# Down projection and next projection with tiles side by side, and the norms between two transformer blocks from one pass of squares

## The chip, the cores and the metric
One core of a Trainium2 chip runs the kernel as one program. The metric is the time of one execution on the device in microseconds (us), the median of the runs shown. TensorE has two clock levels that matter here, 2.4 GHz and 1.2 GHz; the profile gives the level that the chip granted as a share of 2.4 GHz.

## What is computed
Two blocks of a model in float32, width 1024, 256 tokens (the first block has 16 meta tokens ahead of them):

```python
# first block
h = h + concat(hgrn2(u @ w_in), mamba2(u @ w_in)) @ w_out          # u = rmsnorm(h, norm1_w)
h = h + (silu(conv(gate)) * conv(val)) @ ffn_w_down                # gate, val = split(rmsnorm(h, norm2_w) @ ffn_w_up)
x = rmsnorm(h, final_norm_w)
# second block
hc = rmsnorm(ctx, pre_mix_g) * (1 + csc1) + csh1                   # 256 context tokens
hx = rmsnorm(x, pre_mix_g) * (1 + sc1) + sh1
mix = concat(conv_branch(hx @ w_in), retention(hx @ w_in, hc @ w_in)) @ w_out
x = x + g1 * rmsnorm(mix, post_mix_g)
x = x + g2 * rmsnorm(expert_choice_ffn(rmsnorm(x) * (1 + sc2) + sh2), post_ffn_g)   # 16 experts, 24 MB of weights each
```
rmsnorm(x, g) is x * g / sqrt(mean(x * x) + 1e-6). The retention's decays are log_sigmoid(ret_decay_logit), here called the decay work.

## The kernel before
The activations lie with channels on the partitions: the stream is hT, eight tiles (k = 0 to 7) of 128 channels by 272 tokens (258 from the output projection on, 256 from the down projection on; xT(k) is the last 256 tokens of tile k). Each engine has an instruction list of its own, written out by hand, and runs it in order; semaphores join them. The stages, one after the other on TensorE: input projection with both mixers beside it, output projection (tiles ob0 to ob7, oa0 to oa7), norm n2, up projection (44 tiles f0 to f43 of 8 products over k), down projection (tiles d0 to d7), norms n3 and n4, second block's input projection (28 tiles q0 to q27) with the retention between its tiles, output tiles w0 to w7, norms n5 and n6, router, and a loop over 16 experts.

Weights come through a ring of slots of 2 MB; SyncE's queue issues unit u once unit u - 5 is used (`units_used`), in the expert stage six slots are in use. An f unit holds four tiles; the down projection has six units, u_dn[cb][i], for the column halves cb = 0, 1 and the row thirds DK = (0, 8), (8, 16), (16, 22).

From the output projection to q27 every product is made of three (`split_products`, L556): the weights and the activations are split into a rounded part (hi) and the rest (lo), and TensorE adds hi*hi (L566), hi*lo (L567) and lo*hi (L570). The rounded weights are made by ScalarE (`round_weights`, L1036, instruction at L1043), chunk by chunk in the order of the list `chunks` (L386 to L408); four buffers (HB) hold them, so chunk c can be rounded once chunk c - 4 is used (`hi_used`). GpSimd makes the rest in place (L1349, its only work) and signals `w_lo`, for which TensorE waits. An f or q tile is one chunk of 8 k; a down tile k is three chunks d{k}.0, d{k}.1 (8 k each) and d{k}.2 (6 k). The activations' hi is made by ScalarE (`round_stream`, `act_round`), the rest by VectorE (L1690, L1696, L1759).

Result tiles go to three PSUM banks (TB) in the order of the list `seq`: a tile opens once the tile three before it has been read (`tiles_freed`). In the up projection ScalarE reads each tile (L1229), VectorE adds the two other taps of a convolution (L1703, L1704), ScalarE applies silu (L1232), VectorE multiplies (L1708). Added to this, at i = 13 to 20 of 22: TensorE turns the context tokens, ScalarE squares them (L1237) and takes the root (L1240), VectorE computes the gains (L1719), the decay's log chain (L1423 to L1437 at i = 19, with ScalarE's Exp and Ln at L1244, L1246), and the context rows (i = 20: reciprocal L1727, eight scalings L1729, one sum L1731).

In the output and down projections VectorE adds each finished tile to the stream (`add_tile`, L1668) and ScalarE squares it (L1212, L1253). A norm is: eight products of a matrix of 1/1024 with the squares (`norm_sum`, L575, at L581), each float32 product in two passes, the root on ScalarE (`root`, L1052), the reciprocal on VectorE (`inverse_root`, L1358), eight scalings. n2 scales at L1392. Between the blocks two norms follow each other: n3 and the scaling with the final norm's weights (L1748), ScalarE's squares of the result (L1263), n4, and the modulated scaling (L1754), whose hi part is made at L1268.

Of the kernel before, what the change touches and what calls it, by code (L numbers as in the profile page):

```python
# [148 lines left out]
def build(nc, a, out):  # L149
    with ExitStack() as ctx:  # L150
# [38 lines left out]
        eps = sb("eps", [P, 1])  # L189
# [212 lines left out]
        for k in range(KT):  # L402
            for i, (k0, k1) in enumerate(DK):
                u = u_dn[k // 4][i]
                chunk(f"d{k}.{i}", u, kcols(u, k % 4, k1 - k0))
# [15 lines left out]
        seq += [f"f{i}" for i in range(2 * FT)] + [f"d{k}" for k in range(KT)] + ["n3", "n4"]  # L421
# [3 lines left out]
        def bank_of(name):  # L425
            return ps[:, TN[name] % TB, :]
# [102 lines left out]
        def _(pe):  # L529
# [279 lines left out]
            norm_sum("n2", KEPT, lambda k: uT[:, k, 0:KEPT])  # L809
            pe.wait_ge(ev("tiles_freed"), opened[0] - 1)  # L810
            pe.nop().then_inc(ev("out_done"), 1)

            for i in range(FT):
                for s in range(2):
                    o = open_tile(f"f{2 * i + s}")
                    done(split_products(f"f{2 * i + s}", o[:, 0:KEPT], lambda k: uhi2[:, k, :], lambda k: uT[:, k, 0:KEPT],
                                        x_ready=None if i or s else 0))
# [18 lines left out]
            for k in range(KT):  # L836
                cb, m = divmod(k, 4)
                o = open_tile(f"d{k}")
                for i, (k0, k1) in enumerate(DK):
                    if k == 0:  # L840
                        pe.wait_ge(ev("ffn_act"), k1)
                    mm = split_products(f"d{k}.{i}", o[:, 0:L], lambda kk: act_hi[:, kk, :], lambda kk: act_[:, kk, :],
                                        k0, i == 0, i == 2)
                done(mm)
                if m == 3:
                    used(3)
            norm_sum("n3", L, lambda k: uT[:, k, 0:L])

            norm_sum("n4", L, lambda k: uT[:, k, 0:L])

            def in2(r):
# [3 lines left out]
                o = open_tile(f"q{r}")  # L855
                if r == 4:
                    pe.wait_ge(ev("u_tiles"), KT + 1)
                done(split_products(f"q{r}", o[:, 0:width], lambda k: hxhi[:, k, 0:width], lambda k: hx[:, k, 0:width],
                                    x_ready=None if r else 0, ready="mod_tiles"))
# [166 lines left out]
        def _(act):  # L1026
# [25 lines left out]
            def root(name, n):  # L1052

                act.wait_ge(ev("tiles_done"), TN[name] + 1)
                act.activation(bc[:, 0, 0:n], bank_of(name)[:, 0:n], ACT.Sqrt, bias=eps[:]).then_inc(ev("tiles_freed"), 1)
                act.wait_ge(ev("tiles_freed"), TN[name] + 1)
                act.nop().then_inc(ev("root"), 1)
# [82 lines left out]
            def hgrn(j):  # L1140
# [16 lines left out]
                if (j - 32) % 3 == 2:  # L1157
                    act.wait_ge(ev("hg_mean"), h + 1)

                    act.activation(hg_lf, ps[:, 7, 0:T], ACT.Sqrt, bias=eps[:]).then_inc(ev("hg_root"), 1)  # L1160
# [40 lines left out]
            act.activation(bc[:, 0, 0:T], ps[:, 3, 0:T], ACT.Sqrt, bias=eps[:]).then_inc(ev("root"), 1)  # L1201
# [12 lines left out]
            round_weights("f1")  # L1214
# [7 lines left out]
            for i in range(FT):  # L1222
                for s in range(2):
                    m = s * FT + i
                    round_weights((f"f{2 * i + s + 2}", f"d0.{s}")[i == FT - 1])
# [12 lines left out]
                if i == 18:  # L1238
                    act.wait_ge(ev("ctx_mean"), 1)
                    act.activation(bc[:, 0, L:2 * L], ps[:, 6, 0:L], ACT.Sqrt, bias=eps[:]).then_inc(ev("ctx_root"), 1)  # L1240

                if i == 19:
# [724 lines left out]
```

## Time and profile before

| | us |
|---|---|
| runs | 1841.27, 1846.86 (median), 2098.88 |
| profiled execution | 1842.59, its span 1840.7 |
| TensorE products busy in the span | 1429.5 (78%) |
| VectorE, ScalarE, GpSimd busy | 483.4, 439.1, 269.6 |
| mean granted TensorE clock | 0.876 |

Rows of the trace are in us from the start of the span. A row of the chain of waits is start, duration, engine, tensor, line. A row of the timeline is start, busy time, engine, line, operation, operands, count, and in brackets the engine's idle time before it and what ended it.

### The profile page before, as it was taken

How to read it: one execution, taken by the hardware profiler on the slowest of the kernel's cores; microseconds unless marked ns; L12 is line 12 of the kernel's file. 1: busy time of each engine (PE TensorE's matmuls, PEld its weight loads, DVE VectorE, ACT ScalarE, POOL GpSimd, SP SyncE). 2: the span in 40 equal slices, each digit the busy share in tenths (PEclk: the TensorE clock that was granted, in tenths of full speed). 3: DMA queues.
4: the chain of work that ended last, by engine and by line, in shares of the span. 5: the costliest groups of instructions: out<-in, count | busy, mean ns of one | idle time of the engine just before them, and what ended most of it. 6: DMA issues, size and time to landing. Idle time of an engine off the chain costs nothing.

```text
span 1840.7 us, 21118 instructions
## 1 busy us (share of the span) xinstructions
PE 1429.5 (78%) x8673; PEld 881.7 (48%) x8673; DVE 483.4 (26%) x917; ACT 439.1 (24%) x655; POOL 269.6 (15%) x116
## 2 busy tenths in 40 slices
PE   6999899788997879988776677666777676766675
PEld 5777676577997878886522122212222122221221
DVE  3444677644447041583200000000000000000001
ACT  2232555534655343452100000000000000000001
POOL 0000000154884745430000000000000000000000
PEclk9999999889999989999777778788787878887887
DMA  7853443323554332233299999999999999999995
GB/s 253 292 183 142 146 176 112 125 92 120 190 173 161 126 138 92 93 121 154 112 429 429 428 429 428 429 428 429 429 429 428 428 429 428 429 429 429 429 429 246
DMA packets 101115, 523.94 MB, mean 285 GB/s; under 512 B 7961, under 2 KB 30897, under 8 KB 76353
## 3 DMA queue, kind: packets, MB, share of 16 engines
q1 hardware_dynamic: 100841, 523.08, 70.1%
q8 instruction: 40, 0.66, 0.1%
q14 instruction: 18, 0.15, 0.0%
q10 hardware_dynamic: 216, 0.06, 0.0%
HBM read 522.07 MB, written 1.05 MB: 284 GB/s over the span
## 4 chain that ended last, share of the span: by engine, by line
DMA 45%; PE 39%; DVE 10%; ACT 3%; issue 2%; POOL 1%; SPq 0%; DVEq 0%; ACTq 0%; PEldq 0%
DMA ring<-in_w_down 23%; DMA ring<-in_w_up 22%; PE ps L773 8%; PE ps L566 5%; PE ps L570 5%; PE ps L567 5%; PE ps L998 3%; PE ps L1012 2%; PE ps L931 1%; PE ps L553 1%; PE ps L613 1%; DVE arena L1557 1%; PE ps L581 1%; DVE arena L1588 1%; DVE bc L1361 1%
## 5 line engine op out<-in xcount | busy, mean ns | idle before, releaser
L998 PE MATMUL ps<-ring,arena 128*32 128x512 f32 x2048 | 312.2, 760 | 136.7 <-DMA ring<-in_w_up 120.9
L1349 POOL TENSOR_TENSOR ring_r<-ring,ring_r 128x1024 fp32r<-128x1024 f32 (+1 forms) x112 | 269.4, 2418 | 546.9 <-ACT ring_r L1043 546.4
L566 PE MATMUL ps<-arena_r,ring_r 128*128 128x258 f32 (+2 forms) x880 | 271.1, 308 | 45.9 <-POOL ring_r L1349 17.2
L570 PE MATMUL ps<-arena_r,ring_r 128*128 128x258 f32 (+2 forms) x880 | 261.3, 297 | 0.0
L1012 PE MATMUL ps<-ring,arena 128*32 128x512 f32 x1024 | 175.4, 819 | 110.5 <-DMA ring<-in_w_down 103.4
L998 PEld LDWEIGHTS ps<-ring,arena 128*32 128x32 f32 x2048 | 68.7, 130 | 363.2 <-DMA ring<-in_w_up 185.6
L773 PE MATMUL ps<-uT,ring 128*128 128x272 f32 x832 | 206.2, 403 | 3.2 <-DVE uT L1392 3.2
L566 PEld LDWEIGHTS ps<-arena_r,ring_r 128*128 128x128 f32 x880 | 172.3, 196 | 56.5 <-issue 30.7
L773 PEld LDWEIGHTS ps<-uT,ring 128*128 128x128 f32 x832 | 157.7, 194 | 38.0 <-issue 7.1
L570 PEld LDWEIGHTS ps<-arena_r,ring_r 128*128 128x128 f32 x880 | 172.1, 196 | 2.8
L567 PE MATMUL ps<-arena_r,ring_r 128*128 128x256 f32 (+2 forms) x528 | 160.3, 304 | 0.0
L1012 PEld LDWEIGHTS ps<-ring,arena 128*32 128x32 f32 x1024 | 33.2, 131 | 234.8 <-DMA ring<-in_w_down 157.5
L1929 DVE TENSOR_TENSOR arena<-arena,ps 128x512 f32<-128x512 f32 x16 | 11.0, 687 | 437.2 <-PE ps L998 437.2
L1043 ACT ACTIVATE ring_r<-ring 128x1024 fp32r<-128x1024 f32 (+1 forms) x112 | 115.0, 1036 | 25.2 <-PE ps L567 14.8
L567 PEld LDWEIGHTS ps<-arena_r,ring_r 128*128 128x128 f32 x528 | 104.7, 198 | 3.8 <-issue 0.7
L567 PE MATMUL ps<-uT_r,ring_r 128*128 128x258 f32 x352 | 100.8, 286 | 0.0
L553 PE MATMUL ps<-arena 128*128 (+1 forms) x544 | 78.1, 305 | 18.9 <-DVEq L1921 18.9
L553 PEld LDWEIGHTS ps<-arena 128*128 128x128 f32 x544 | 75.6, 221 | 31.4 <-issue 31.4
L1931 DVE COPY arena<-ps 128x512 f32<-128x512 f32 x16 | 11.1, 692 | 301.3 <-PE ps L1012 301.3
L1328 ACT ACTIVATE arena<-ps 128x512 f32<-128x512 f32 x16 | 9.6, 597 | 313.0 <-PE ps L998 313.0
L1330 ACT ACTIVATE arena<-ps 128x512 f32<-128x512 f32 x16 | 9.6, 597 | 297.7 <-PE ps L1003 297.7
L1018 PE MATMUL ps<-arena 128*128 128x512 f32 x128 | 64.8, 653 | 14.3 <-DVEq L1934 14.3
(331 smaller groups left out, 1336.9 us busy)
## 6 DMA issues: line engine op xcount, KB each, us to landing
ring<-in_w_gate SPq DMA_DIRECT2D x64, 2048.0 KB, 26.0
ring<-in_w_up SPq DMA_DIRECT2D x64, 2048.0 KB, 19.7
ring<-in_w_down SPq DMA_DIRECT2D x64, 2048.0 KB, 25.7
ring<-in_w_in SPq DMA_DIRECT2D x20, 2048.0 KB, 12.1
ring<-in_w_ada SPq DMA_DIRECT2D x12, 2048.0 KB, 8.5
ring<-in_ffn_w_up SPq DMA_DIRECT2D x22, 1024.0 KB, 7.3
ring<-in_w_out SPq DMA_DIRECT2D x6, 2048.0 KB, 8.7
ring<-in_ffn_w_down SPq DMA_DIRECT2D x4, 2048.0 KB, 8.3
```

The lines of the kernel that those rows point to most:

```text
L553: mm = pe.matmul(o, l, r, start=i == 0, stop=i == len(pairs) - 1)
L566: pe.matmul(o, hi[:, k, :], r_(xhi(k0 + k)), start=first and k == 0, stop=False)
L567: mm = pe.matmul(o, hi[:, k, :], r_(xlo(k0 + k)), start=False, stop=False)
L570: mm = pe.matmul(o, lo[:, k, :], r_(xhi(k0 + k)), start=False, stop=last and k == nk - 1)
L581: mm = pe.matmul(o[:, 0:n], w[:], src(k), start=k == 0, stop=k == nk - 1)
L613: mm = pe.matmul(ps[32 * j:32 * j + 32, 3, :], cond[:, k, :], w[:, k, :], start=k < 4, stop=k >= 4)
L773: mm = pe.matmul(o[:, 0:T], w[:, k, :], uT[:, k, :], start=k == 0, stop=k == KT - 1)
L998: mm = pe.matmul(ps[32 * j:32 * j + 32, half, :], xs[:, kt, :], w[:, k, 512 * j:512 * j + 512], start=kt == 0, stop=kt == KT - 1)
L1012: mm = pe.matmul(ps[32 * j:32 * j + 32, half, :], heT[:, j, 32 * i:32 * i + 32], w[:, j, 512 * half:512 * half + 512], start=i == 0, stop= ...
L1018: mm = pe.matmul(ps[:, 4 + b, :], Gt[:, w * P:w * P + P], ye[:, half * 512:half * 512 + 512], start=False, stop=False, skip_group_check=True)
L1043: act.activation(r_(rounded(c)), chunks[c][1], ACT.Copy).then_inc(ev("w_hi"), 1)
L1349: pool.tensor_tensor(r_(w), w, f_(rounded(c)), ALU.subtract).then_inc(ev("w_lo"), 1)
```

## The change
The diff's core. It orders the down projection's chunks by `DOWN`: in each half of four tiles, three tiles side by side over the row thirds, then the fourth. f0 to f2 and q0 to q2 are computed side by side over k. The norms n2, n3 and n4 are made of two products each: VectorE adds up the squares of tiles 0 to 6, and the last tile's squares are the second product. n4 is no longer computed from the scaled stream: ScalarE squares the stream with the magnitudes of the final norm's weights as scale (small[:, 216:224]), n4 comes before n3, with 1e-12 under its root, and the gain of q's input includes those weights (small[:, 208:216]). The stream's own scaling follows after q's input. The log chain and the context rows are moved from the up projection into the down projection, the rounding of f0 to f2 ahead of n2's last squares.

```diff
+        DOWN = [(k, i) for k0 in (0, 4) for ks in (range(k0, k0 + 3), [k0 + 3]) for i in range(3) for k in ks]
...
# TensorE
-            norm_sum("n2", KEPT, lambda k: uT[:, k, 0:KEPT])
+            def last_sums(name, width, acc, last):
+                o = open_tile(name)
+                pe.matmul(o[:, 0:width], ones[:], acc, start=True, stop=False)
+                squares[0] += 1
+                pe.wait_ge(ev("squares"), squares[0])
+                done(pe.matmul(o[:, 0:width], ones[:], last, start=False, stop=True))
+            squares[0] += KT - 1
+            pe.wait_ge(ev("norm2_sums"), 1)
+            last_sums("n2", KEPT, uT[:, 0, 0:KEPT], uT[:, KT - 1, 0:KEPT])
...
+            def side_by_side(names, width, xhi, xlo, ready):
+                tiles = [open_tile(name) for name in names]
+                for k in range(KT):
+                    pe.wait_ge(ev(ready), k + 1)
+                    for name, o in zip(names, tiles):
+                        mm = split_products(name, o[:, 0:width], xhi, xlo, first=k == 0, last=k == KT - 1, ks=[k])
+                        if k == KT - 1:
+                            done(mm)
+            side_by_side(["f0", "f1", "f2"], KEPT, lambda k: uhi2[:, k, :], lambda k: uT[:, k, 0:KEPT], "u_tiles")
...
-            for k in range(KT):
-                cb, m = divmod(k, 4)
-                o = open_tile(f"d{k}")
-                for i, (k0, k1) in enumerate(DK):
...
-                if m == 3:
-                    used(3)
-            norm_sum("n3", L, lambda k: uT[:, k, 0:L])
-            norm_sum("n4", L, lambda k: uT[:, k, 0:L])
+            for k, i in DOWN:
+                if i == 0:
+                    open_tile(f"d{k}")
...
+                if i == 2:
+                    done(mm)
+                    if k % 4 == 3:
+                        used()
+                elif k % 4 == 3:
+                    mm.then_inc(ev("units_used"), 1)
+            squares[0] += 2 * (KT - 1)
+            pe.wait_ge(ev("stream_sums"), 1)
+            last_sums("n4", L, hx[:, 0, 0:L], hx[:, KT - 1, 0:L])
+            last_sums("n3", L, uT[:, 0, 0:L], uT[:, KT - 1, 0:L])
...
+                if r == 0:
+                    side_by_side(["q0", "q1", "q2"], L, lambda k: hxhi[:, k, 0:L], lambda k: hx[:, k, 0:L], "mod_tiles")
...
# ScalarE
             for k in range(KT):
+                if k >= 5:
+                    round_weights(f"f{k - 5}")
                 act.wait_ge(ev("stream_tiles"), 2 * KT + k + 1)
                 act.activation(uT[:, k, 0:KEPT], hT[:, k, KEPT0:T], ACT.Square).then_inc(ev("squares"), 1)
...
+            def stream_squares(k):
+                act.wait_ge(ev("stream_tiles"), 3 * KT + k + 1)
+                act.activation(hx[:, k, 0:L], xT(k), ACT.Square, scale=small[:, 216 + k:217 + k]).then_inc(ev("squares"), 1)
+                act.activation(uT[:, k, 0:L], xT(k), ACT.Square).then_inc(ev("squares"), 1)
+            for n, (k, i) in enumerate(DOWN):
+                round_weights(f"d{k}.{i}")
+                if n == 4:
                     act.wait_ge(ev("lg_abs"), 1)
                     act.activation(small[:, 40:48], small[:, 32:40], ACT.Exp, scale=-1.0).then_inc(ev("lg_exp"), 1)
+                if n == 6:
                     act.wait_ge(ev("lg_one"), 1)
                     act.activation(small[:, 56:64], small[:, 48:56], ACT.Ln).then_inc(ev("lg_log"), 1)
...
+                if n >= 3 and DOWN[n - 3][1] == 2:
+                    stream_squares(DOWN[n - 3][0])
+            round_weights("q2")
+            stream_squares(KT - 1)
+            root("n4", L, 0, 1)
+            root("n3", L, L)
             for k in range(KT):
                 act.wait_ge(ev("mod_scaled"), k + 1)
                 act.activation(r_(hxhi[:, k, 0:L]), hx[:, k, 0:L], ACT.Identity, bias=mod[:, k, 0:1]).then_inc(ev("u_hi"), 1)
+            act.activation(r_(hxhi[:, :, L:2 * L]), hx[:, :, L:2 * L], ACT.Copy).then_inc(ev("u_hi"), 1)
...
# VectorE
                 add_tile(f"oa{k}", k, KEPT0)
+                if 1 <= k < KT - 1:
+                    dve.wait_ge(ev("squares"), 2 * KT + k + 1)
+                    ins = tt(uT[:, 0, 0:KEPT], uT[:, 0, 0:KEPT], uT[:, k, 0:KEPT], ALU.add)
...
             for k in range(KT):
                 add_tile(f"d{k}", k, META)
+                if 1 <= k < KT - 1:
+                    dve.wait_ge(ev("squares"), 3 * KT + 2 * k + 2)
+                    st(tt(hx[:, 0, 0:L], hx[:, 0, 0:L], hx[:, k, 0:L], ALU.add))
+                    st(tt(uT[:, 0, 0:L], uT[:, 0, 0:L], uT[:, k, 0:L], ALU.add))
+                    st.wait()
+                if k == 2:
+                    context_rows()
+                if k == KT - 2:
+                    dve.nop().then_inc(ev("stream_sums"), 1)
             inverse_root(L)
-            for k in range(KT):
-                stt(xT(k), xT(k), pc("fin", k), bc[:, 1, 0:L], ALU.mult, ALU.mult).then_inc(ev("x_tiles"), 1)
-            inverse_root(L)
...
```
`context_rows` holds the lines L1726 to L1731 of before; the log chain stands just ahead of this loop.

## Rows read from the trace of the kernel before

**Rows 1.** The page: DMA share in 40 slices of the span, and GpSimd's group
```profile
DMA  7853443323554332233299999999999999999995
...
L1349 POOL TENSOR_TENSOR ring_r<-ring,ring_r 128x1024 fp32r<-128x1024 f32 (+1 forms) x112 | 269.4, 2418 | 546.9 <-ACT ring_r L1043 546.4
```

**Rows 2.** The chain of waits, two pieces of the expert stage
```profile
915.37 24.53 DMA ring<-in_w_down
...
939.95 3.35 PE ps L1012 x16
...
943.31 25.99 DMA ring<-in_w_up
```

**Rows 3.** Windows: PE, PEld, DVE, ACT, POOL busy (count), granted clock, DMA
```profile
440.00:460.00 20.00, 18.82 (x134) 18.49 (x135) 12.90 (x26) 13.57 (x22) 12.18 (x6) 0.87 0.19 60
460.00:480.00 20.00, 19.39 (x160) 19.04 (x159) 9.35 (x22) 11.74 (x21) 16.80 (x7) 1.00 0.60 204
```

**Rows 4.** The chain of waits at norm n2
```profile
429.75 3.73 PE ps L581 x16
...
434.06 1.78 DVE bc L1361
...
435.86 4.54 DVE uT L1392 x2
```

**Rows 5.** Timeline of TensorE: starts of f0, f4, f40, d0.0, d0.2, d4.2, q0, q4
```profile
440.88 0.55 PE L566 MATMUL ps<-arena_r,ring_r 128*128 128x258 f32 x1 [7.42 <-DVE uT_r L1690]
...
455.39 0.36 PE L566 MATMUL ps<-arena_r,ring_r 128*128 128x258 f32 x1 [0.30 <-PE ps L570]
...
568.89 0.36 PE L566 MATMUL ps<-arena_r,ring_r 128*128 128x258 f32 x1 [0.30 <-PE ps L570]
...
585.89 0.36 PE L566 MATMUL ps<-arena_r,ring_r 128*128 128x256 f32 x1 [0.62 <-POOL ring_r L1349]
...
599.46 0.55 PE L566 MATMUL ps<-arena_r,ring_r 128*128 128x256 f32 x1 [7.61 <-POOL ring_r L1349]
...
636.52 0.58 PE L566 MATMUL ps<-arena_r,ring_r 128*128 128x256 f32 x1 [3.34 <-POOL ring_r L1349]
...
683.48 0.36 PE L566 MATMUL ps<-arena_r,ring_r 128*128 128x256 f32 x1 [4.07 <-DVE arena_r L1759]
...
699.57 0.47 PE L566 MATMUL ps<-arena_r,ring_r 128*128 128x512 f32 x1 [0.30 <-PE ps L570]
```

**Rows 6.** Timeline of GpSimd
```profile
435.29 4.83 POOL L1349 TENSOR_TENSOR ring_r<-ring,ring_r 128x1024 fp32r<-128x1024 f32 x2 [14.29 <-ACT ring_r L1043]
...
575.29 4.67 POOL L1349 TENSOR_TENSOR ring_r<-ring,ring_r 128x1024 fp32r<-128x1024 f32 x2 [5.59 <-ACT ring_r L1043]
...
604.93 6.56 POOL L1349 TENSOR_TENSOR ring_r<-ring,ring_r 128x768 fp32r<-128x768 f32 x3 [0.94 <-ACT ring_r L1043]
...
671.74 4.84 POOL L1349 TENSOR_TENSOR ring_r<-ring,ring_r 128x1024 fp32r<-128x1024 f32 x2 [11.86 <-ACT ring_r L1043]
```

**Rows 7.** The chain of waits, log chain and context rows
```profile
577.70 2.30 DVE small L1437
...
585.20 5.76 DVE arena L1729 x8
...
590.98 2.30 DVE arena L1731
```

**Rows 8.** The chain of waits from the down projection to q0
```profile
670.56 6.32 DVE hT L1748 x5
...
680.00 1.76 DVE bc L1361
```

**Rows 9.** Timelines of VectorE and ScalarE at the last down tile
```profile
664.22 0.42 DVE L1672 TENSOR_TENSOR hT<-hT,ps 128x256 f32<-128x256 f32 x1 [7.50 <-PE ps L570]
...
664.73 0.42 ACT L1253 ACTIVATE uT<-hT 128x256 f32<-128x256 f32 x1 [6.76 <-DVEq L1674]
...
665.16 1.28 ACT L1055 ACT_TABLE_LOAD   x1
```

More of the change, by code:

```diff
@@ L420, in build @@
         seq += [f"ob{k}" for k in range(KT)] + [f"oa{k}" for k in range(KT)] + ["n2"]
-        seq += [f"f{i}" for i in range(2 * FT)] + [f"d{k}" for k in range(KT)] + ["n3", "n4"]
+        seq += [f"f{i}" for i in range(2 * FT)] + [f"d{k}" for k in range(KT)] + ["n4", "n3"]
         seq += [f"q{j}" for j in range(28)] + [f"w{k}" for k in range(KT)] + ["n5", "n6"]
@@ L1200, in _ @@
             act.wait_ge(ev("mz1_done"), 1)
-            act.activation(bc[:, 0, 0:T], ps[:, 3, 0:T], ACT.Sqrt, bias=eps[:]).then_inc(ev("root"), 1)
+            act.activation(bc[:, 0, 0:T], ps[:, 3, 0:T], ACT.Sqrt, bias=eps[:, 0:1]).then_inc(ev("root"), 1)
             m2_round(1)
@@ L1244, in _ @@
                     act.activation(small[:, 40:48], small[:, 32:40], ACT.Exp, scale=-1.0).then_inc(ev("lg_exp"), 1)
+                if n == 6:
                     act.wait_ge(ev("lg_one"), 1)
                     act.activation(small[:, 56:64], small[:, 48:56], ACT.Ln).then_inc(ev("lg_log"), 1)
-            act_round(FT - 1)
-            round_weights("d0.2")
-            for k in range(KT):
-                if k < KT - 1:
-                    round_weights(f"d{k + 1}.1")
-                act.wait_ge(ev("stream_tiles"), 3 * KT + k + 1)
-                act.activation(uT[:, k, 0:L], xT(k), ACT.Square).then_inc(ev("squares"), 1)
-                if k < KT - 1:
-                    round_weights(f"d{k + 1}.2")
@@ L1256, in _ @@
-            root("n3", L)
-            act.activation(r_(hxhi[:, :, L:2 * L]), hx[:, :, L:2 * L], ACT.Copy).then_inc(ev("u_hi"), 1)
-            round_weights("q1")
-            for k in range(KT):
-                act.wait_ge(ev("x_tiles"), k + 1)
-                act.activation(uT[:, k, 0:L], xT(k), ACT.Square).then_inc(ev("squares"), 1)
-            root("n4", L)
+                if n >= 3 and DOWN[n - 3][1] == 2:
+                    stream_squares(DOWN[n - 3][0])
+            round_weights("q2")
@@ L1366, in _ @@
             st(dve.memset(ones1[:], 1.0 / P))
[L1367 removed]
+            st(dve.memset(eps[:, 0:1], 1e-6))
+            st(dve.memset(eps[:, 1:2], 1e-12))
             st.wait()
@@ L1719, in _ @@
                         st(stt(gain[:, :, c], mod[:, 8:16, c], 1.0, pc("prem", 0, 8), ALU.add, ALU.mult))
[L1720 to L1729 removed]
                     st.wait()
[L1731 removed]
+                    st(tt(small[:, 208:216], gain[:, :, 0], pc("fin", 0, 8), ALU.mult))
             act_rest(FT - 1)
@@ L1741, in ret_args, with context_rows @@
                 dve.nop().then_inc(ev("ret_arg"), 1)
+            lgt = bcast8[:, 24:32]
+            log1p_of_exp(lgt, small[:, 40:48], small[:, 48:56], small[:, 56:64], small[:, 32:40], "lg_abs", "lg_exp", "lg_one", "lg_log")
+            st.link(stt(small[:, 80:88], lgt, 0.0, small[:, 56:64], ALU.min, ALU.subtract))
+            def context_rows():
+                dve.wait_ge(ev("ctx_root"), 1)
+                st.link(dve.reciprocal(bc[:, 1, L:2 * L], bc[:, 0, L:2 * L]))
+                for k in range(KT):
+                    st(stt(hx[:, k, L:2 * L], hx[:, k, L:2 * L], gain[:, k, 1:2], bc[:, 1, L:2 * L], ALU.mult, ALU.mult))
+                st.wait()
+                st.link(tt(hx[:, :, L:2 * L], hx[:, :, L:2 * L], mod[:, 0:8, 1:2].to_broadcast([P, KT, L]), ALU.add))
@@ L1763, in _ @@
+            dve.wait_ge(ev("root"), roots[0])
+            st.link(dve.reciprocal(bc[:, 1, L:2 * L], bc[:, 0, L:2 * L]))
+            for k in range(KT):
+                stt(xT(k), xT(k), pc("fin", k), bc[:, 1, L:2 * L], ALU.mult, ALU.mult).then_inc(ev("x_tiles"), 1)
             dve.wait_ge(ev("dist_loaded"), 16)
```

75 lines of the change are left out of this document (36 added, 39 removed).

## The prediction
> **What bounds the kernel now.** The page's slices come first. From slice 21 on the DMA engines are busy over 90% of the time, and before it they are mostly idle [rows 1]. The chain of waits says the same of its second half: a transfer of some 25 us, 3 us of TensorE, the next transfer [rows 2]. So the expert stage runs at the pace of its weights, and nothing in the diff touches it. The first 900 us are computation. At their end the ring of six slots has long been full and waits for the first expert, so whatever the first part saves, the end should save too: the same transfers start earlier. I therefore look only for the time at which TensorE reaches fixed places. The timeline of TensorE's starts gives them [rows 5]: up projection tile f0 at 440.88, f4 at 455.39, f40 at 568.89, down projection at 585.89, first tile of the next projection (q0) at 683.48, q4 at 699.57. A tile of 24 products takes 2.88 us at the full clock: from 460 to 480 us 160 products run in 20 us at granted clock 1.00, 2.4 GHz, 0.12 us each with 0.3 us every fourth tile [rows 3].
>
> **Part 1, the norm ahead of the up projection.** Before, the last output tile ends at 429.5; sixteen passes of the sum of squares (L581) take 3.73 us, the root 0.5, the reciprocal 1.78, and then two scalings take 4.54 us and hold f0 until 440.88 [rows 4, 5]. Two scalings cost 0.9 us elsewhere; here GpSimd works from 435.29 to 440.12 on f0 and f1 (4.83 us, two operations), and VectorE's second scaling ends only when it does [rows 6]. In the new kernel VectorE adds squares 0 to 6 beside TensorE's output tiles, so after the last square (at 430.4) only one product of 0.5 us is left, not eight: the root comes at 431.0 instead of 433.5. And f0, f1 and f2 are rounded during the last output tiles, so GpSimd is idle when the scaling begins. Reciprocal until 433.3, first scaling, rounding and rest 1.3 us: f0 starts at 434.7, 6.2 us earlier.
> Then f0, f1 and f2 run side by side: 72 products. TensorE idles 3.7 us ahead of them. After the old idle it ran at 1.2 GHz for 4.4 us (mean grant 0.87 from 440 to 460 [rows 3]); I take 4 us of that again: 19 products at 0.21 and 53 at 0.12, together 10.5 us, until 445.2. What is late next is f3. Its rounding stands behind f0's eviction in ScalarE's order, and f0 now ends at 444.5, last but two. Eviction 0.55, rounding 1.05, GpSimd 2.42 (the mean of its line [rows 1]): f3 starts at 448.6 and f4 at 452.0. Gain at f4: 455.4 - 452.0 = **3.4 us**. With the clock kept at 2.4 GHz it would be 5.3; with two more blocked sums in front of the norm, about 1.
>
> **Part 2, context rows and decay leave the up projection.** From f40 to the down projection the old kernel needs 585.89 - 568.89 = 17.0 us for four tiles that need 12.0. ScalarE's and VectorE's log chain stands ahead of f42's rounding, with eight-element operations of 2.3 us each [rows 7]. Without it: **5.0 us**. What it leaves behind (a product of eight gains, one more root of eight numbers) runs on engines with some 4 us of slack for a freed bank; zero, at most 2.4 us if one of them meets GpSimd and the slack is not there.
>
> **Part 3, the down projection.** Its 24 chunks are 16 of 2.88 us and 8 of 2.16 us, 63.4 us, with two hand-overs 64.0. Before, it lasts from 585.89 to 664.2, 78.3 us. The excess of 14.3 us is the start of d0.2 at 599.46 (7.6 us idle: the last activation tiles came behind the 8 us of context rows, 585.20 to 593.3 [rows 5, 7]), the wait for the last weight unit until 636.52 (3.3 us idle: all three units of the first half were given back at once), and 2.5 us of low clock after each. All of it goes. The order with three tiles side by side puts d0.2 17.3 us after the start, so the last activation tiles have time; the first unit is given back after d3.0, 22 us ahead of the transfer's use. **14.3 us.**
> But the work comes back here. The context rows (a reciprocal 1.75, eight scalings, a sum of 2.3 us) now stand on VectorE between the add of d2 and the add of d3; behind d3's add stand the bank that d6.0 wants and, on ScalarE, d3's squares and the rounding of all chunks after d6.0. In the down projection GpSimd works 6.56 us for every 7.92 us (three operations [rows 6]), and rows show what VectorE does beside it: 8-element operation 2.30 us while GpSimd runs two operations from 575.29 to 579.96 [rows 6, 7]; five of eight stream scalings 6.32 us, while GpSimd runs from 671.74 to 676.58 [rows 6, 8]. VectorE gets in one operation with two SBUF inputs per operation of GpSimd. The working, with the down projection starting at 577.5 (568.9 - 3.4 + 12.0): the tail of the log chain meets GpSimd until about 598.7, so d0 is added 1.7 us late; the first two sums of squares wait for it too; d4.0's weights come 1.5 us late. Context rows begin at 608.0, three scalings get in by 616.7 between GpSimd's three last chunks, then GpSimd has nothing (ScalarE waits for d3), the other five take 1.9 and the sum 2.3: 620.9. d3 is added at 621.4, d6.0 starts at 621.5 instead of 616.6 (4.9), and the chunk after it waits for rounding and GpSimd (1.4). Sum **-7.8 us**. Bounds: 0, if VectorE is never held (context rows then take 7 us, less than the 8.6 us of chunks in hand), and -17, if every sum and every scaling pays a whole operation of GpSimd. I take -7.8 as it follows the pattern of the rows that are nearest. The down projection then ends at 577.5 + 64.0 + 7.8 = 649.3.
> The Trainium skill says of this ("SBUF — State Buffer", section "SBUF: two separate sides") that VectorE with two SBUF inputs and GpSimd share a port pair as an exclusive lock, held for the whole instruction. It speaks against the change's place for the context rows, and the trace agrees (2.30 us for eight elements). Without such a lock this term would be 0 and the time about 1810.
>
> **Part 4, the norms between the blocks.** Before, from the last down product (664.2) to q0 (683.48): 19.3 us with two sums of squares, two roots, two reciprocals and the stream scalings between them [rows 8]. New, from that end T: add 0.3 to 0.7, squares until 1.6, table load 1.28 (the old one starts right behind the square [rows 9]), root until 3.4, reciprocal until 5.3, scaling, rounding and rest 1.7 as before (680.00 + 1.76 to 683.48): q0 at T + 7.0. GpSimd's q2 is done by T + 5, so nothing holds the scalings. **12.3 us.** q0 to q2 side by side then take 10.5 us as above, until T + 17.5; q3 again waits for eviction, rounding and GpSimd until T + 21.0; q4 starts at T + 24.3, 17.3 us after q0 where it was 16.1: **-1.1 us**. The stream's own scaling (a reciprocal and eight operations) is moved behind the products, where VectorE is free until the rotations; 0. The context's rest, 2.3 us, is done by T + 16.4, ahead of q4. The three weight units that the old kernel asks for at 664.3 are asked for from T - 5 on; they are wanted at T + 24 and later.
>
> **Sum.** 3.4 + 5.0 + 14.3 - 7.8 + 12.3 - 1.1 = 26.1 us. The profiled execution took 1842.59 (span 1840.7 and 1.9 around it): 1816.5. Two of the runs shown are 1841.27 and 1846.86 (the median, 4.3 above the profiled one), their mean 1.5 above it. Forecast: **1818 us**, a chance of 0.5; its own range 1812 to 1824.
>
> **Rivals.**
> *VectorE is not held in the down projection* (0.25). For: chunks are rounded up to four ahead, so there are gaps. Against: the 2.30 us of an 8-element operation. Time 1818 - 7.8 = 1810; with the clock kept in part 1 too, 1808.
> *The lock bites further* (0.13): sums, log chain and context rows each meet GpSimd, -17 instead of -7.8: 1827.
> *The expert transfers hide it* (0.07): the stage is bound by DMA, and if its transfers were what is full already, the end would stay: 1843. Against: slices 19 and 20 of the DMA row are 3 and 2 tenths [rows 1], so the bound begins after the first expert's start.
> *Slower than before* (0.05): ScalarE runs in order, and each stream square now stands ahead of the weights' rounding. If a tile's two sums each lose a whole operation of GpSimd (2 x 2.8), then with add, two squares, rounding and GpSimd 5.6 + 0.4 + 0.8 + 1.05 + 2.4 = 10.3 us stand against 7.9 us of products: 2.4 us on each of six tiles, 14 us; and context rows at 8 x 2.8 + 4 = 26 us against 6 us of cover lose 20 us where I count 4.9, 15 more. 1818 + 14 + 15 = 1847. It decides from the point at which GpSimd is never idle for a whole chunk; the profile shows 1.4 us of idle in 7.9.
>
> **Chances.** The range: 1806 to 1832; what stays outside is the third and fourth rival and tails. A measurement of this kernel tells about 2% from no change, 37 us, that is below 1810 or above 1884. Faster by over 2%: the first rival's better half and a little, 0.15. Slower by over 2%: 0.01. Within: 0.84.
>
> **What would show it.** f0 at about 434.7 with a last product of squares at 430.5, f3 released by GpSimd at about 448.6, f4 at 452. No wait between f40 and the down projection at 577.5. In the down projection no wait on a weight transfer, but one of some 5 us at about 617 on VectorE (d6.0, with the bank of d3), VectorE's context scalings at 2.8 us for each of the first three. The end of the down projection to q0: 7 us. Wrong would be: no wait at d6.0 (first rival), waits at several tiles (second), or a stage from f4 to f40 that is not as long as before (113.5 us), or an expert stage longer than before.

## The result, and the profile after

The changed kernel takes **1821.38 us** in the median of four runs (1820.54 to 1821.69), beside 1847.09 us for the kernel before on the same chip (four runs, 1841.27 to 2098.88): a ratio of 0.9873 with a 95% interval of 0.9854 to 0.9891, so 1.1 to 1.5% less time, inside the 2% to which the forecast gave 0.84. The ratio leaves out the one slow run, of 2098.88 us. The forecast was 1818 us with 1806 to 1832 around it. The profiled execution took 1821.69 us (span 1819.9), where the profiled one of before took 1842.59 (1840.7): 20.8 us of span, where the sum said 26.1.

The page of the changed kernel first, the DMA share in 40 slices:

```profile
DMA  7853443423654342323599999999999999999995
```

GpSimd's work is what it was in [rows 1], 112 operations of 2.42 us. The DMA row is full from slice 21 on, as before; slice 20, which had 2 tenths, has 5. The expert stage only starts earlier, with the same transfer of some 25 us, then 3 us of TensorE.

Where the time went is read from TensorE's starts (columns: start, us, engine, line, operation, in brackets the idle time ahead of it and who ended it). Changed kernel: output tiles oa4 and oa5, n2's products, f0, f3, f4, f40, d0.0, d6.0, the two norms, q0, q3, q4:

```profile
417.32 0.36 PE L567 MATMUL ps<-arena_r,ring_r 128*128 128x258 f32 x1 [0.30 <-PE ps L571]
...
421.32 0.39 PE L567 MATMUL ps<-arena_r,ring_r 128*128 128x258 f32 x1 [0.90 <-DVE hT L1704]
...
430.96 0.70 PE L813 MATMUL ps<-uT,ones 128*128 128x258 f32 x2 [0.77 <-DVE uT L1717]
...
436.61 0.55 PE L567 MATMUL ps<-arena_r,ring_r 128*128 128x258 f32 x1 [4.11 <-DVE uT_r L1728]
...
451.08 0.36 PE L567 MATMUL ps<-arena_r,ring_r 128*128 128x258 f32 x1 [3.40 <-POOL ring_r L1380]
...
456.02 0.36 PE L567 MATMUL ps<-arena_r,ring_r 128*128 128x258 f32 x1 [0.30 <-PE ps L571]
...
569.31 0.36 PE L567 MATMUL ps<-arena_r,ring_r 128*128 128x258 f32 x1 [0.30 <-PE ps L571]
...
581.54 0.36 PE L567 MATMUL ps<-arena_r,ring_r 128*128 128x256 f32 x1 [0.30 <-DVEq L1743]
...
623.25 0.58 PE L567 MATMUL ps<-arena_r,ring_r 128*128 128x256 f32 x1 [3.56 <-DVE hT L1704]
...
652.37 0.67 PE L813 MATMUL ps<-arena,ones 128*128 128x256 f32 x2 [0.30 <-PE ps L571]
...
658.88 0.36 PE L567 MATMUL ps<-arena_r,ring_r 128*128 128x256 f32 x1 [4.14 <-DVE arena_r L1804]
...
672.99 0.36 PE L567 MATMUL ps<-arena_r,ring_r 128*128 128x256 f32 x1 [3.81 <-POOL ring_r L1380]
...
677.90 0.48 PE L567 MATMUL ps<-arena_r,ring_r 128*128 128x512 f32 x1 [0.30 <-POOL ring_r L1380]
```

A product's start less its idle bracket is the end of the one before. So oa7 ends at 430.96 - 0.77 = 430.19, and the last down product, T, at 652.37 - 0.30 = 652.07. Against [rows 5]:

| stage, us | before | predicted | after |
|---|---|---|---|
| end of oa7 to f4 | 25.9 | 22.6 | 25.8 |
| f4 to f40 | 113.5 | 113.5 | 113.3 |
| f40 to d0.0 | 17.0 | 12.0 | 12.2 |
| d0.0 to T | 78.3 | 71.8 | 70.5 |
| T to q0 | 19.3 | 7.0 | 6.8 |
| q0 to q4 | 16.1 | 17.3 | 19.0 |

oa7 itself ends 0.7 us later than before. Its group of four tiles, oa4 to oa7, starts 0.5 us earlier (417.32) than in the kernel before:

```profile
417.79 0.36 PE L566 MATMUL ps<-arena_r,ring_r 128*128 128x258 f32 x1 [0.30 <-PE ps L570]
```

It lasts 430.19 - 417.32 = 12.9 us where it took 429.45 - 417.79 = 11.7: 1.2 us are lost there, most of them at oa5, which waits 0.90 us for the add that frees its bank. At q4 the gain is 699.57 - 677.90 = 21.7 us.

There are three waits of 3.4 to 3.8 us in these rows (f3, d6.0, q3); in the kernel before, f3 and d6.0 do not wait at all, and q3 waits 1.05. What follows each is in the windows of the changed kernel (columns as in [rows 3]):

```profile
623.00:627.00 4.00, 3.75 (x17) 3.76 (x18) 0.95 (x3) 3.66 (x5) 1.88 (x1) 0.50 0.54 198
627.00:632.00 5.00, 5.00 (x36) 5.00 (x35) 0.00 (x0) 0.96 (x2) 5.00 (x3) 0.77 0.01 3
...
672.90:677.90 5.00, 4.62 (x25) 4.47 (x25) 5.00 (x3) 0.51 (x2) 4.97 (x2) 0.66 0.01 3
```

TensorE works on without a gap from 623 us, but at granted clock 0.50, 1.2 GHz, for 4 us and at 0.77 for the next 5: (1 - 0.50) x 4 + (1 - 0.77) x 5 = 3.1 us on top of the wait, an estimate from the grants. For q3 the grant is 0.66 over the tile. In f3 and q3 the fall comes inside the tile: the first products of f3 start 0.12 us apart, and from 451.9 to 455.1 0.21, so the tile lasts 456.02 - 0.30 - 451.08 = 4.6 us and not 2.88.

Why f3 waits is plain from ScalarE and GpSimd. ScalarE (f0's eviction, f3's rounding), changed kernel:

```profile
447.00 0.56 ACT L1259 ACTIVATE arena<-ps,par 128x256 f32<-128x256 f32 x1 [6.12 <-PE ps L571]
447.47 1.04 ACT L1072 ACTIVATE ring_r<-ring 128x1024 fp32r<-128x1024 f32 x1
```

GpSimd, the rest of f3 and the operations beside the context rows further down, changed kernel:

```profile
448.59 2.35 POOL L1380 TENSOR_TENSOR ring_r<-ring,ring_r 128x1024 fp32r<-128x1024 f32 x1 [15.48 <-ACT ring_r L1072]
...
610.70 7.45 POOL L1380 TENSOR_TENSOR ring_r<-ring,ring_r 128x1024 fp32r<-128x1024 f32 x3 [2.68 <-ACT ring_r L1072]
```

With three tiles side by side f0 ends with the last but two of 72 products. Until then ScalarE stood 6.12 us at the eviction with f3's rounding queued behind it, and GpSimd 15.48 us.

VectorE, changed kernel: the first sum of n2, three operations of the log chain, the context rows, the add of d3:

```profile
418.70 2.10 DVE L1717 TENSOR_TENSOR uT<-uT 128x258 f32<-128x258 f32 x1 [6.96 <-ACT uT L1243]
...
586.36 2.35 DVE L1457 SCALAR_TENSOR_TENSOR small<-bcast 128x8 f32<-128x8 f32 x1
589.04 2.03 DVE L1460 TENSOR_SCALAR small<-small 128x8 f32<-128x8 f32 x1 [0.33 <-ACT small L1285]
...
595.25 0.20 DVE L1465 RECIPROCAL small<-small 128x8 f32<-128x8 f32 x1
...
612.29 8.12 DVE L1781 SCALAR_TENSOR_TENSOR arena<-arena,small,bc 128x256 f32<-128x256 f32 x8
...
622.77 0.42 DVE L1704 TENSOR_TENSOR hT<-hT,ps 128x256 f32<-128x256 f32 x1
```

The context rows stand ahead of the add that frees d6.0's bank, as forecast, and d6.0 starts 0.5 us after that add's start.

### The profile page after: what moved, and what is told of

Same layout as the page of the kernel before. It is cut to its first block, busy times and chain, and to the rows that moved or that the text cites. A ratio compares the mean times of both kernels' runs of the same rounds, so it can differ in the third digit from the quotient of the medians.

```text
span 1819.9 us, 21088 instructions
## 1 busy us (share of the span) xinstructions
PE 1420.7 (78%) x8637; PEld 874.8 (48%) x8637; DVE 508.8 (28%) x938; ACT 438.2 (24%) x655; POOL 270.0 (15%) x116
## 3 DMA queue, kind: packets, MB, share of 16 engines
HBM read 522.07 MB, written 1.05 MB: 287 GB/s over the span
## 4 chain that ended last, share of the span: by engine, by line
DMA 45%; PE 39%; DVE 10%; ACT 3%; issue 2%; POOL 1%; SPq 0%; DVEq 0%; ACTq 0%
DMA ring<-in_w_down 23%; DMA ring<-in_w_up 22%; PE ps L774 7%; PE ps L567 5%; PE ps L571 5%; PE ps L568 5%; PE ps L1027 3%; PE ps L1041 3%; PE ps L960 1%; PE ps L554 1%; PE ps L614 1%; DVE arena L1589 1%; POOL ring_r L1380 1%; DVE arena L1620 1%; PE ps L705 1%
## 5 line engine op out<-in xcount | busy, mean ns | idle before, releaser
L1982 DVE COPY arena<-ps 128x512 f32<-128x512 f32 x16 | 11.1, 692 | 303.8 <-PE ps L1041 303.8
L1359 ACT ACTIVATE arena<-ps 128x512 f32<-128x512 f32 x16 | 9.6, 597 | 314.9 <-PE ps L1027 314.9
L1361 ACT ACTIVATE arena<-ps 128x512 f32<-128x512 f32 x16 | 9.6, 597 | 293.6 <-PE ps L1032 293.6
L1363 ACT ACTIVATE arena<-ps 128x512 f32<-128x512 f32 x16 | 9.6, 597 | 279.6 <-PE ps L1041 279.6
## 6 DMA issues: line engine op xcount, KB each, us to landing
ring<-in_w_in SPq DMA_DIRECT2D x20, 2048.0 KB, 11.7
```

## The experiments

All ratios are against the kernel before, run beside each on the same chip. The unchanged opening of the program shifts by some 3 us either way from run to run (n2's products start between 428.7 and 435.2), so stages are compared by their length.

**1. The fourth tile's weights rounded ahead of f0's eviction.** The fourth buffer is free all along.

```diff
             round_stream(uhi2, 1, KEPT)
+            round_weights("f3")
...
+            round_weights("q3")
             act.activation(r_(hxhi[:, :, L:2 * L]), hx[:, :, L:2 * L], ACT.Copy)
```

> f3 and q3 are rounded ahead of the first evictions. My theory (their late weights, and the low clock after the wait, ate the side-by-side gain): f3 starts at 447.4 instead of 451.1 and runs at 0.12 us a product, f4 at 450.5 instead of 456.0; q4 some 4 to 5 us earlier on top; time 1811 to 1813. Rival (the clock is low there whatever comes before, and GpSimd only blocks VectorE elsewhere): less than 4 us in all, 1818 or more.

Measured: 1815.16 us (1813.24 to 1816.09), ratio 0.9831 (0.9809 to 0.9853). TensorE in this run, f3 and f4:

```profile
449.66 0.39 PE L567 MATMUL ps<-arena_r,ring_r 128*128 128x258 f32 x1 [1.04 <-DVEq L1745]
...
454.25 0.36 PE L567 MATMUL ps<-arena_r,ring_r 128*128 128x258 f32 x1 [1.44 <-POOL ring_r L1382]
```

End of oa7 to f4 is 23.3 us, q0 to q4 14.3. The wait on GpSimd at f3 is gone, but f3 now waits 1.0 us for f0's bank, and f4 1.4 for GpSimd. f4 comes 2.5 us earlier behind oa7 where I expected 5.5, q4 4.7 us earlier on top as expected. Part of the loss was the rounding's place; the rest stays, because f0's bank and buffer come free late anyway.

**2. f0 to f2 and q0 to q2 one after another**, all else as changed.

```diff
-            side_by_side(["f0", "f1", "f2"], KEPT, ...)
+            for nm in ("f0", "f1", "f2"):
+                side_by_side([nm], KEPT, ...)
```

and the same for q0 to q2.

> f0 to f2 and q0 to q2 one after the other, all else as changed. My theory: f0 ends at 442, so f3's weights come in time and f4 starts at about 451 (5 us earlier); q0 to q4 takes 16.1 us as before instead of 19.0; time 1813 to 1815. Rival (side by side saves the waits for k): 3 to 5 us slower, 1825.

Measured: 1811.85 us (1808.98 to 1812.04), ratio 0.9816 (0.9796 to 0.9837). ScalarE in this run, f0's eviction (f3's rounding starts right behind it, at 440.71):

```profile
440.24 0.56 ACT L1261 ACTIVATE arena<-ps,par 128x256 f32<-128x256 f32 x1 [1.64 <-PE ps L571]
```

Windows of this run, f0 to f3:

```profile
434.00:440.00 6.00, 5.82 (x24) 5.74 (x25) 4.92 (x14) 2.52 (x6) 0.00 (x0) 0.50 0.26 81
440.00:450.00 10.00, 9.70 (x80) 9.52 (x80) 3.82 (x9) 7.25 (x12) 5.90 (x3) 0.99 0.01 2
```

f0 starts at 434.18 and is evicted 6.1 us later (in the changed kernel 10.4). f3 has its weights in time, nothing waits, and the clock stays up behind f0's slow first tile. End of oa7 to f4: 21.2 us instead of 25.8; q0 to q4: 14.8 instead of 19.0. Side by side costs 4.6 + 4.2 = 8.8 us. The single step of this study that pays most is to take it out.

**3. The context rows one tile later.**

```diff
-                if k == 2:
+                if k == 3:
                     context_rows()
```

> The context rows stand behind d3's add instead of d2's. If they cost what the wait at d6.0 and the low clock after it show, this wait (3.6 us) is gone and the down projection takes 65 to 66 us instead of 70.5, time about 1816. Rival: GpSimd is never idle behind d3, the scalings take 2.8 us each, and d4's add is late instead: no change, 1821.

Measured: 1817.76 us (1817.63 to 1823.05), ratio 0.9848 (0.9827 to 0.9869). VectorE in this run:

```profile
622.62 1.75 DVE L1779 RECIPROCAL bc<-bc 128x256 f32<-128x256 f32 x1
624.40 12.54 DVE L1781 SCALAR_TENSOR_TENSOR arena<-arena,small,bc 128x256 f32<-128x256 f32 x8
636.98 4.37 DVE L1783 TENSOR_TENSOR arena<-arena,mod 128x2048 f32<-128x2048 f32 x1
```

GpSimd in this run:

```profile
615.00 20.86 POOL L1380 TENSOR_TENSOR ring_r<-ring,ring_r 128x1024 fp32r<-128x1024 f32 x9 [2.67 <-ACT ring_r L1072]
```

The window of its down projection:

```profile
585.80:651.50 65.70, 64.18 (x528) 63.50 (x528) 49.10 (x45) 32.09 (x46) 51.64 (x24) 1.00 0.47 174
```

The wait at d6.0 is gone, and with it the low clock: 65.7 us against 70.5, grant 1.00, as my theory had it. The gain is read from the stage; the ratio's interval overlaps that of the changed kernel (0.9854 to 0.9891). Yet the context rows themselves take longer, 12.5 us for eight scalings instead of 8.1, and the sum 4.4 instead of 2.3: GpSimd works without a gap until 615.00 + 20.86 = 635.86, of which 11.5 us beside the scalings, five of its operations of 2.3 us. One scaling gets in for each (11.5), and the last ones take 0.4 each. Their length is not what costs; where they stand is. From T to q0 it takes 7.9 us here (6.8).

**4. The old norm n2 put back**, and with it the old places of the rounding of f0 to f2.

```diff
-                if k >= 5:
-                    round_weights(f"f{k - 5}")
...
+            norm_sum("n2", KEPT, lambda k: uT[:, k, 0:KEPT])
```

> Norm n2 as eight products again and no early rounding of f0 to f2; the rest as changed. Old root and blocked scaling: f0 at 440.3 instead of 436.6; side by side then until 451, f4 at 459.5: 3.5 us slower, 1825. Rival (VectorE's sums held back the output tiles as much as they saved): 1821 or less.

Measured: 1833.19 us (1830.65 to 1837.13), ratio 0.9927 (0.9903 to 0.9951), 8 us above what was expected. TensorE in this run:

```profile
453.29 0.58 PE L567 MATMUL ps<-arena_r,ring_r 128*128 128x258 f32 x1 [6.07 <-POOL ring_r L1377]
```

f2 is rounded at its old place, behind f0's eviction, but side by side it is wanted with f0: TensorE waits 6.07 us in the middle of the three. So this kernel prices two things at once and says nothing of the norm; experiment 12 does it with the tiles in sequence.

**5. Log chain and context rows back in the up projection** (i = 19 and i = 20), the rest as changed.

```diff
+                if i == 19:
+                    ... log1p_of_exp(...)
+                if i == 20:
+                    ... reciprocal, eight scalings, sum
...
-                if k == 2:
-                    context_rows()
```

> Log chain and context rows back in the up projection (i = 19 and 20), the rest as changed. f40 to the down projection takes 17 us again instead of 12.2, but the down projection loses its waits (64 to 65 us instead of 70.5): 0 to 2 us faster than the changed kernel, about 1820. Rival (the move itself is a gain): 5 us slower, 1826 or more.

Measured: 1827.96 us (1827.11 to 1834.03), ratio 0.9916 (0.9887 to 0.9946). TensorE in this run, f42, d0.0, d1.0:

```profile
579.04 0.55 PE L567 MATMUL ps<-arena_r,ring_r 128*128 128x258 f32 x1 [2.90 <-POOL ring_r L1379]
...
587.16 0.36 PE L567 MATMUL ps<-arena_r,ring_r 128*128 128x256 f32 x1 [0.75 <-POOL ring_r L1379]
...
595.68 0.58 PE L567 MATMUL ps<-arena_r,ring_r 128*128 128x256 f32 x1 [5.44 <-DVEq L1742]
```

f40 to d0.0 is back at 17.0 us, as before; the 5.0 of part 2 are shown. My theory, that the down projection would give most of it back, missed: the new order opens its second tile one chunk after the first, that tile wants the bank of f42, and VectorE reads it only behind the context rows, so d1.0 waits 5.4 us. The new order needs the move; whether the move needs the new order is asked in experiment 6. By the stages the moves are worth 4.8 us ahead of d0.0 and 0.9 behind it, 6.6 us between the medians, although they bring the wait at d6.0.

**6. The down projection tile by tile again**, the rest as changed.

```diff
-        DOWN = [(k, i) for k0 in (0, 4) for ks in (range(k0, k0 + 3), [k0 + 3]) for i in range(3) for k in ks]
+        DOWN = [(k, i) for k in range(KT) for i in range(3)]
```

> Down projection tile by tile again (Ln right after Exp, for the order's sake), the units still given back one by one, the rest as changed. My theory: with the moves made, d0.2's activations are ready in time, and d3's bank is wanted three tiles later than before, so the context rows cost nothing: the down projection takes 65 us instead of 70.5, time about 1816. Rival (the side-by-side order is what removed the old stall): d0.2 waits again 5 us or more, 1821 to 1827.

Measured: 1823.03 us (1820.74 to 1826.76), ratio 0.9887 (0.986 to 0.9914). Its down projection lasts 69.6 us (70.5). TensorE in this run, d2.0 and d5.0:

```profile
598.67 0.36 PE L567 MATMUL ps<-arena_r,ring_r 128*128 128x256 f32 x1 [1.74 <-POOL ring_r L1378]
...
626.43 0.36 PE L567 MATMUL ps<-arena_r,ring_r 128*128 128x256 f32 x1 [3.29 <-POOL ring_r L1378]
```

ScalarE ahead of d3's squares, and the window of the down projection:

```profile
622.09 0.51 ACT L1277 ACTIVATE arena<-hT,small 128x256 f32<-128x256 f32 x1 [4.72 <-DVEq L1704]
...
580.86:650.42 69.56, 64.22 (x528) 63.48 (x528) 38.73 (x44) 32.94 (x47) 55.49 (x26) 1.00 0.43 155
```

Neither side had it: d0.2 did not wait for its activations, and it was not faster either. Two other waits, for GpSimd's rest of the weights, come in their place, and both lead back to the moved work. d3's products end at 614.7, but VectorE adds d3 at 621.58, behind the context rows (612.42 to 621.55); ScalarE stands 4.72 us for that add, and d5.0's rounding is next after d3's squares. In the same way d0's add (593.80) stands behind the log chain, and d2.0's rounding behind d0's squares. So the context rows cost a wait of some 3 us in this order too. No low clock follows it, though: behind the 3.29 us of idle the products start 0.12 us apart from the second on, and the grant is 1.00 over the whole stage. With the context rows out of the up projection, the order of the down projection is worth nothing that these runs resolve.

**7. The context scalings with one operand from PSUM.**

```diff
-   st(stt(hx[:, k, L:2 * L], hx[:, k, L:2 * L], gain[:, k, 1:2], bc[:, 1, L:2 * L], ALU.mult, ALU.mult))
+   st(stt(hx[:, k, L:2 * L], ps[:, 4 + k % 2, 0:L], gain[:, k, 1:2], bc[:, 1, L:2 * L], ALU.mult, ALU.mult))
```

> The eight context scalings read their data from PSUM instead of SBUF (other data, so q's context half is not the model's), so each has one SBUF tensor input less; everything else as changed. If VectorE is held because it and GpSimd both want two SBUF inputs, the eight take 3 to 4 us instead of 8.1 and the wait at d6.0 shrinks from 3.6 us to nothing, down projection 66 us. Rival (the scalings are slow for their shape, or for the sync between engines): 8 us and the wait stay.

Measured: 1812.12 us in one run, so only its trace is compared. VectorE in this run:

```profile
609.84 3.23 DVE L1781 SCALAR_TENSOR_TENSOR arena<-ps,small,bc 128x256 f32<-128x256 f32 x8
613.10 4.40 DVE L1783 TENSOR_TENSOR arena<-arena,mod 128x2048 f32<-128x2048 f32 x1
```

GpSimd in this run:

```profile
608.25 7.11 POOL L1380 TENSOR_TENSOR ring_r<-ring,ring_r 128x1024 fp32r<-128x1024 f32 x3 [2.67 <-ACT ring_r L1072]
```

The same eight operations take 3.23 us instead of 8.12 beside the same three of GpSimd. The sum behind them, still with two operands from SBUF, meets the third and takes 4.40 instead of 2.29, its time in the changed kernel. So what holds VectorE is where its operands come from, and it is that instruction, not its engine, that waits for GpSimd. d6.0 then waits 0.78 us, and the down projection lasts 66.6.

**8. The context rows spread over five tiles**: reciprocal and two scalings behind d2, two each behind d3, d4 and d5, the sum behind d6.

```diff
-                if k == 2:
-                    context_rows()
+                if 2 <= k <= 6:
+                    context_rows(k - 2)
```

> The context rows are spread: reciprocal and two scalings behind d2's add, two more behind d3, d4 and d5 each, the sum behind d6. No block is longer than the cover of two or three chunks: no wait at d6.0, down projection 65 us instead of 70.5, nothing late at the norms: time about 1816. Rival (late sums push d7's add and the norm back): the stage behind it loses as much, 1820.

Measured: 1820.15 us (1814.47 to 1826.37), ratio 0.9874 (0.9825 to 0.9922). The window of its down projection:

```profile
581.50:645.60 64.10, 63.76 (x528) 63.44 (x528) 43.96 (x44) 31.11 (x46) 50.47 (x23) 1.00 0.46 168
```

TensorE in this run, the norms and q0:

```profile
647.97 0.70 PE L813 MATMUL ps<-arena,ones 128*128 128x256 f32 x2 [2.33 <-DVEq L1798]
...
656.26 0.55 PE L567 MATMUL ps<-arena_r,ring_r 128*128 128x256 f32 x1 [4.99 <-DVE arena_r L1807]
```

The 64.0 us that part 3 counts for the bare products are reached, 6.4 less than with the change. But T to q0 takes 10.6 us instead of 6.8: the sum stands ahead of d7's add and of the signal for the norms' first product (2.3 us of idle), and GpSimd, later in its work, meets the first scalings. 3.8 of the 6.4 us are given back, and the ratio's interval is too wide to show the 2.6 that are left. The time is the rival's 1820.

**9 and 10. Combinations.** Experiments 2 and 8 together; then f in sequence, q side by side with q3 rounded early, and the spread rows.

> Sequential first tiles and spread context rows together. If the two costs are independent: f4 4.6 us earlier, q0 to q4 4.2 us shorter, down projection 5 us shorter than in the changed kernel: 1821.4 - 13.8 = 1808.

> f0 to f2 one after the other, q0 to q2 side by side with q3 rounded early, context rows spread. q0 to q4 took 14.3 us in the run with early rounding and 14.8 in the sequential one, so this should be within 1 us of the one before: 1807 to 1809.

Measured: 1811.29 us (1809.67 to 1816.93), ratio 0.9831 (0.9789 to 0.9873), and 1812.22 (1810.21 to 1815.57), ratio 0.9823 (0.9783 to 0.9862). Both are 3 us or more above what was expected, and neither beats experiment 2: both still have the sum ahead of the last add, and wait 2.3 us for it at the norms.

**11. All of it together.** Tiles in sequence, two scalings behind each of d2 to d5, and the sum and its rounding moved behind q's input.

```diff
+                if 2 <= k <= 5:
+                    context_rows(k - 2)
...
+            context_rows(4)
+            dve.nop().then_inc(ev("ctx_rows"), 1)
```

> First tiles one after the other; two context scalings behind each of d2 to d5; their sum of 2.3 us behind q's inputs, its rounding behind q1's eviction. The down projection should keep the 64.1 us of the spread run, and the norms their 6.8 us to q0 instead of 10.6; q4 some 15 us after q0. That is 21 us less of stages than before plus 4.6 at the first tiles: about 1805. Rival (the context's rest comes too late for q4): 1808.

Measured: **1808.9 us** (1807.41 to 1812.31, five runs), ratio 0.9803 (0.9788 to 0.9817): below the changed kernel's interval altogether, though not apart from experiment 2's (0.9796 to 0.9837), and 4 us above what was expected. TensorE in this run, d0.0, the norms, q0, q4:

```profile
577.27 0.36 PE L567 MATMUL ps<-arena_r,ring_r 128*128 128x256 f32 x1 [0.30 <-DVEq L1747]
...
641.64 0.67 PE L813 MATMUL ps<-arena,ones 128*128 128x256 f32 x2 [0.30 <-PE ps L571]
643.73 0.70 PE L816 MATMUL ps<-arena,ones 128*128 128x256 f32 x2 [1.42 <-ACT arena L1280]
...
649.87 0.36 PE L567 MATMUL ps<-arena_r,ring_r 128*128 128x256 f32 x1 [4.58 <-issue]
...
666.77 0.47 PE L567 MATMUL ps<-arena_r,ring_r 128*128 128x512 f32 x1 [1.46 <-POOL ring_r L1384]
```

The down projection takes 64.1 us, T to q0 8.5 (ScalarE squares d7 only behind three roundings, hence the 1.42), q0 to q4 16.9: 89.5 us from d0.0 to q4, against 96.4 in the changed kernel and 91.1 in experiment 2. So over experiment 2 it gains 1.6 us by the stages, and the times do not resolve that.

**12. The old norm n2 put back, tiles in sequence.** The edit of experiment 4 on the kernel of experiment 2.

> First tiles one after the other and norm n2 as in the kernel before, the rest as changed: against the sequential run only the norm's part is gone. From the last output product to f4 that run took 21.2 us, the kernel before 25.9: so 4.7 us slower than 1811.9, 1816 to 1817. Rival (VectorE's sums gain nothing): 1812.

Measured: 1817.71 us (1814.52 to 1819.94), ratio 0.9854 (0.9834 to 0.9875), 5.9 us above experiment 2 in the medians. TensorE in this run, the old sums, f0, f4:

```profile
430.38 3.72 PE L582 MATMUL ps<-uT,ones 128*128 128x258 f32 x16 [0.30 <-PE ps L571]
441.46 0.56 PE L567 MATMUL ps<-arena_r,ring_r 128*128 128x258 f32 x1 [7.36 <-DVE uT_r L1721]
...
455.93 0.36 PE L567 MATMUL ps<-arena_r,ring_r 128*128 128x258 f32 x1 [0.30 <-POOL ring_r L1379]
```

From oa7's end, 430.38 - 0.30, to f4: 25.85 us, what the kernel before has, and 21.2 with the new norm in sequence. The new norm, with the early rounding of f0 to f2, is worth 4.6 us there, and the side-by-side tiles spend just that. Ahead of oa7's end it costs 1.2: oa4 to oa7 take 12.9 us in experiment 2 (415.05 to 427.91) and 11.7 here (418.38 to 430.08). Net 3.5 us are left.

## Why the prediction was right or wrong

The sum said 26.1 us; at q4 it was 21.7, and of these 0.9 are lost up to the end of the span. The forecast of 1818 is 3.4 us below the median. Right in sum, with one thing left out that comes three times.

**Part 1 (3.4 us predicted, 0.1 measured, and 1.2 lost ahead of it) is the step that failed.** By its pieces, from oa7's end: f0 at 6.4 us where I had 5.2; the three tiles 11.1 us where I had 10.5; f3's wait 3.4 where I had 3.4; f3 to f4 4.9 where I had 3.4. Two things were missing. First, I took VectorE's sums to lie "beside TensorE's output tiles" at no cost. They stand in VectorE's order ahead of adds that free banks. The first waits 6.96 us for squares that ScalarE makes behind the rounding of oa7; they stood there in the kernel before too, but nothing wanted them ahead of the norm. It then takes 2.10 us beside GpSimd's rest of oa7, the add of oa2 comes behind it, and oa5 starts 0.9 us late. Three of the six sums take 0.4 us; the last two take 2.3 and 1.5 us beside the rest of f0 and f1, and from oa7's end the root comes 0.9 us and f0 1.2 us later than in the working. The prediction had named this case ("with two more blocked sums in front of the norm, about 1") and not taken it. Second, and more: the wait at f3 I found, with its cause and its length, but I let f3 run at the full clock behind it. It ran at 1.2 GHz from its seventh product on, 1.8 us. What the "clock kept at 2.4 GHz" alternative asked was only whether the clock comes back after f0; whether it falls again after f3's wait was not asked. Experiment 2 shows both at once: no wait, no second fall, 4.6 us.

**Part 2 (5.0 predicted) was right.** 17.0 became 12.2, and experiment 5 brings the 17.0 back. The reason, log chain ahead of f42's rounding, shows there as f42's 2.90 us.

**Part 3 (14.3 less 7.8 predicted, 7.8 gained) was near in sum by luck, with a wrong make-up.** The excess went: no wait for a weight transfer, none at d0.2. What came back is 70.5 - 64.0 = 6.5 us where I had 7.8. The one wait is where it was forecast, at d6.0, on the add of d3; it is 3.6 us, 3.3 more than a hand-over, where I had 4.9. The chunk after it does not wait (I had 1.4), nor do the log chain's held operations delay d4.0 (I had 1.5). In their place stand 3.1 us of low clock behind the wait, which I had not priced: 3.3 + 3.1 = 6.4. The 4.5 us charged for what did not come cover the 3.1 left out. I had read just such "2.5 us of low clock after each" into the old kernel's waits, and credited their removal, but charged none to the new wait. With the wait gone (experiments 3 and 8) the clock is 1.00 throughout and the stage takes 65.7 and 64.1 us.

That VectorE with two SBUF operands waits for GpSimd's whole instruction is shown by experiment 7: 8.12 us against 3.23 with one operand from PSUM. By the rule of the Trainium skill ("SBUF — State Buffer", section "SBUF: two separate sides") the shared port pair is an exclusive lock for the whole instruction; the trace agrees. Held operations behave as in [rows 6, 7], so the rival in which VectorE is not held (1810) is out. So is the one in which the lock bites further (1827): the log chain is held, and so are the sums behind d1 and d5 (1.6 and 2.1, 1.5 and 2.1 us where those of the other tiles take 0.4), but no wait of TensorE comes of them. Of the context rows, GpSimd is done at 610.70 + 7.45 = 618.15, so three of the eight scalings are held and five run free, which is the working of part 3.

**Part 4: 12.3 predicted, 12.5 measured; then -1.1 predicted, -2.9 measured.** The norms from one pass are as forecast within 0.2 us. q0 to q4 repeats f0 to f4: q3 waits 3.81 us, is at low clock behind it, and 1.8 us more are gone than I had.

**Expert stage.** The rival in which its transfers hide the gain fell: 21.7 us at q4 arrive as 20.8 at the end. The slower-than-before rival needed GpSimd never idle for a whole chunk; experiment 3 comes close (nine operations without a gap, 12.5 us for eight scalings), and even there nothing waits but 1.2 us, as the banks' slack covers it.

What stays open: why the clock stays up behind the 3.29 us of idle in experiment 6 and falls behind the 3.56 of the changed kernel; where the 0.9 us between q4 and the end of the span go; and what of the new norm's gain is the early rounding's. 11's q0 to q4 is 2.1 us longer than experiment 2's: q4 waits 1.46 us, its weights' rounding standing behind that of the context rows, and the grant is 0.66 from q0 to 660.0 where it is 0.82 in experiment 2 over the like stretch. No run parts the two.

## What to carry to other kernels

Interleaving tiles delays the first tile's end, and with it everything queued behind its eviction: when tiles are put side by side at the start of a stage, follow the fourth tile's weights, not the first three. To a new wait of 3 to 4 us on TensorE the slow stretch behind it is to be added as a second charge that may come or not: here 3.56 us of idle cost 6.4, but in experiment 6 3.29 us cost no more than themselves. And filler work on VectorE belongs in pieces behind the adds that free banks, and none of it ahead of the last add before a norm; this last is shown by the stages' lengths (experiments 8 and 11), not by the times.

## What was not expected of the hardware

- The clock need not fall at once: behind f3's 3.40 us of idle the first seven products start 0.12 to 0.19 us apart, then the spacing is 0.21 until three products before the tile's end. Behind d6.0's 3.56 us it is 0.21 from the second product on. Behind waits of 1.0 and 1.4 us (experiment 1) it does not fall: the grant is 1.00 from 449.7 to 458.0. Nor does it in the down projections of experiments 3 and 8, whose longest wait is 1.2 us, nor in that of experiment 6, with a wait of 3.29 us. So the length of the wait alone does not tell it.
- Of the log chain's eight-element operations, TENSOR_SCALAR, with one tensor operand, is held too (2.03, 1.77 and 1.86 us, where it takes 0.17 in the kernel before with GpSimd idle), while the one RECIPROCAL takes 0.20. It did not just find a gap between two of GpSimd's operations: in experiment 3 the reciprocal of 256 elements takes its usual 1.75 us (622.62 to 624.37) while GpSimd works without a gap. So RECIPROCAL, also with one tensor operand, is not held.
- The share between VectorE and GpSimd is one operation for one even with GpSimd's next ones queued without a gap (experiment 3): neither starves the other, and what VectorE waits depends on the number of its held instructions, not on their size. Eight elements take as long (2.35 us) as 256 (2.0 to 2.6).
